# HGRN head: one half chunk of projection taken from behind level 4 and put in front of level 0

## The chip, the cores and the metric

The kernel runs on one core of a Trainium2 chip. The metric is the device time of one execution, in microseconds (us), as the median of several runs. A "head" below is one of the eight HGRN heads, a "half" is half of the matmuls of one chunk of a projection.

## What is computed

The program is one layer of a decoder trunk: RMSNorm, one wide projection of 1024 prompt tokens and 64 sample tokens, dilated attention, HGRN2, causal pooling, gates, and an output projection. The change lies in the HGRN2 part alone. Cut to what matters:

```python
f = lb + (1.0 - lb) * jax.nn.sigmoid(bfg)      # forget gate, 8 heads x 128
logf, kin = jnp.log(f), 1.0 - f
# per head, chunkwise: decay between positions s <= t
decay = exp(cumsum(logf)[t] - cumsum(logf)[s])
att = einsum('btk,btsk,bsk->bts', q, decay, kin)
o = att @ v + (q * exp(A)) @ S                 # S: 128 x 128 state
o_b = rmsnorm(o) * silu(bg)
```

## The kernel before

All tokens lie along the free axis as features x 1088 tokens, in three chunks of 384, 384 and 320 tokens. A projection of one feature block of 128 columns is a *unit*: for each chunk 24 matmuls, since weights and activations are split in a high and a low part (`w_hi` with `x_hi` and `x_lo`, then `w_lo` with `x_hi`). A chunk can be cut in two halves of 12 matmuls; the first half holds the first 12 of them, the second half the other 12, and the third chunk's second half ends the unit.

The weights of a unit are split by GpSimd: a cast into `w_hi` (L206) and a subtraction into `w_lo` (L208), both from SBUF to SBUF, 128x1024 elements. There are two slots, used in turn; GpSimd may split the weights of unit u only when TensorE has finished unit u-2, whose slot they take (the wait on `proj_done` in `split`). So a split starts whenever a unit ends.

A head has four units to project for the *next* head (forget gate, q, v, output gate: `j` = 0 to 3), 24 halves in all, and its own small products: the rows of v transposed (`v_rows`), eight levels of block products (`product(i, n)`, L1341, 34 matmuls of 128x32 in levels 1 to 3 and 32 in levels 4 to 6), the rows of k (`k_rows`), states, outputs, and the transposition back. TensorE runs them in an order written out by hand: `head` places so many halves behind each product. The tuple `counts` says how many: in front of level 0, behind each of the levels 0 to 7, then four numbers for the later places. The queue of every engine is in order.

VectorE serves the levels. Behind the product of level n it runs `update(n)`: it multiplies the decays into `b_block_decay` (L1503), `b_q_decayed` (L1505) and `b_k_decayed` (L1507), and the last of the three releases the product of level n+1. Level 0 has a single multiplication in its place. Then comes `take(n)`, which copies the product out of PSUM (L1486). Between `take(3)` and `update(4)` two more operations stand in VectorE's queue: `b_v_own` (L1527) and `b_q_own` (L1531). All of L1503, L1505, L1507, L1527 and L1531 have both inputs and the output in SBUF; L1486 reads PSUM.

The eight heads are seven turns of a hardware loop and the last head written out by itself, with its own counts.

Of the kernel before, what the change touches and what calls it, by code (L numbers as in the profile page):

```python
# [106 lines left out]
def build(nc, A, OUT):  # L107
    ctx = ExitStack()
    with ctx:
# [1044 lines left out]
        def hgrn_phase(ext, p_gate, p_graw, then):  # L1154
# [10 lines left out]
            with scope:  # L1165
# [71 lines left out]
                with nc.Block() as block:  # L1237
# [86 lines left out]
                    def _(pe):  # L1324
                        def product(i, n):

                            if n == 0:
                                cv.emptied(pe, i * UNITS + 1)
                            pe.wait_ge(level_ready, i * 9 + 1 + n)
                            q = q_new if n == 0 else qp  # L1330
                            for m, (b0, nb, w) in enumerate(level_uses(n)):
                                bank = cv.fill(pe, i * MISC, M[f"p{n}"] + m, w < P or n == LEVELS - 1)
                                for b in range(nb):
                                    t0 = (b0 + b) * P
                                    if n == LEVELS - 1:
                                        mm = pe.matmul(bank[0:HP, b * HP:(b + 1) * HP], kr[:, t0:t0 + HP],
                                                       second(q[:, t0:t0 + P], n), start=True, stop=True)
                                        continue
                                    wq = HP if n == 0 else HP // 2
                                    for r in range(0, w, HP):  # L1340
                                        mm = pe.matmul(bank[r:r + HP, b * wq:(b + 1) * wq], kr[:, t0 + r:t0 + r + HP],  # L1341
                                                       second(q[:, t0 + r:t0 + r + HP], n), start=True, stop=True)
                                mm.then_inc(cv.misc_done, 1)
# [36 lines left out]
                        def outputs(i):  # L1380
                            pe.wait_ge(states_ready, i + 1)
                            for q in range(2):
                                bank = cv.fill(pe, i * MISC, M["o"] + q)
                                for b in range(4):
                                    t = 4 * q + b
                                    mm = pe.matmul(bank[:, b * P:(b + 1) * P], att[:, t, :], vrow[:, t, :],
                                                   start=True, stop=(t == 0))
                                    if t > 0:
                                        mm = pe.matmul(bank[:, b * P:(b + 1) * P], qp[:, t * P:(t + 1) * P],
                                                       state[:, t, :], start=False, stop=True)  # L1390
                                mm.then_inc(cv.misc_done, 1)

                        def back(i):
                            pe.wait_ge(o_ready, i + 1)
                            for q, (b0, nb) in enumerate(spans):
                                bank = cv.fill(pe, i * MISC, M["y"] + q, q == 2)
                                w = P if q < 2 else NS
                                for b in range(nb):
                                    mm = pe.transpose(bank[:, b * P:b * P + w], osb[0:w, b0 + b, :],
                                                      ident[0:w, 0:w])  # L1400
                                mm.then_inc(cv.misc_done, 1)

                        def v_rows(i):
                            cv.emptied(pe, i * UNITS + 2)
                            rows_of(i, v_new, M["v"])

                        def k_rows(i):
                            pe.wait_ge(level_ready, i * 9 + 9)
                            rows_of(i, kr, M["k"])
# [5 lines left out]
                        def head(i, counts):  # L1415

                            halves = [(j, c, half) for j in range(UNITS) for c in range(NCH) for half in range(2)]

                            def meanwhile(n):
                                for j, c, half in halves[:n]:  # L1420
                                    cv.project(pe, i * UNITS + (UNITS + j), j % 2, c, KO, x_hi, x_lo, half=half)
                                del halves[:n]

                            before, levels, own, out, turn, after = counts
                            v_rows(i)
                            meanwhile(before)
                            for n in range(LEVELS):
                                product(i, n)
                                meanwhile(levels[n])
                            k_rows(i)  # L1430
                            meanwhile(own)
                            own_states(i)
                            meanwhile(out)
                            outputs(i)
                            meanwhile(turn)
                            back(i)
                            meanwhile(after)
                            assert not halves

                        with pe.Fori(0, BH - 1) as i:  # L1440
                            head(i, (1, (1, 1, 1, 1, 2, 1, 1, 1), 2, 4, 5, 3))
                        head(BH - 1, (1, (1, 1, 1, 1, 2, 1, 1, 1), 3, 5, 6, 0))
                        for c in range(NCH - 1):
                            cv.project(pe, BH * UNITS + len(POOL_AT), 0, c, KO, x_hi, x_lo)
# [1068 lines left out]
```

## Time and profile before

| | |
|---|---|
| median of 3 runs | 1928.43 us (1927.81 to 1932.0) |
| the profiled execution | 1930.2 us, span 1928.4 us |
| TensorE, matmul records busy | 1886.4 us, 98% of the span |
| VectorE busy | 726.8 us, 38% |
| GpSimd busy | 460.1 us, 24% |
| mean granted TensorE clock | 0.996 |
| the HGRN part | about 715 to 1265 us of the span; one head is 69.2 us |

Idle time is read as follows: a row of a timeline names in brackets how long the engine had stood idle before that group of instructions, and what released it. "issue" means that the profile shows nothing that it waited for. PE is TensorE's matmuls, PEld its weight loads, DVE is VectorE, POOL is GpSimd.

### The profile page before, as it was taken

To read this page: it belongs to the slowest core of one execution; us is meant where nothing else is said; L and a number is where in the kernel's file an instruction comes from. 1 tells how busy PE (TensorE), PEld (TensorE's weight loads), DVE (VectorE), ACT (ScalarE), POOL (GpSimd) and SP (SyncE) were. 2 spreads that over 40 slices of the span, in tenths; PEclk is the share of its full clock that TensorE was granted. 3 is DMA by queue.
4 is the path that set the end of the run, shared out by engine and by line. 5 is a ranking of instruction groups with operands and counts; after the bars stand their busy time and mean duration, and the time that the engine had idled before them with its cause. 6 is when DMAs were issued, how large, how long until landed. Compare 5 with 4: busy or idle time off the path is not lost. (4 is left out here: it accounts for less than half of the span.)

```text
span 1928.4 us, 34551 instructions
## 1 busy us (share of the span) xinstructions
PE 1886.4 (98%) x13648; PEld 1814.0 (94%) x13648; DVE 726.8 (38%) x1271; ACT 355.9 (18%) x876; POOL 460.1 (24%) x266
## 2 busy tenths in 40 slices
PE   7999999999999999999999999999999999999898
PEld 6999998999999999999999999998999999999897
DVE  6223123123222316655755664657200132211523
ACT  5121121122022110111011011122111221111321
POOL 2321222122122121222212222132333333333300
PEclk9999999999999999999999999999999999999999
DMA  5424315322432330221121122123422232212522
GB/s 157 112 68 93 111 53 109 89 74 48 127 92 63 76 94 23 68 67 39 50 67 45 55 66 61 32 79 144 134 68 67 79 103 84 84 56 84 206 89 88
DMA packets 240804, 159.25 MB, mean 83 GB/s; under 512 B 35277, under 2 KB 226125, under 8 KB 240716
## 3 DMA queue, kind: packets, MB, share of 16 engines
q1 hardware_dynamic: 202844, 124.16, 22.7%
q10 hardware_dynamic: 37872, 33.79, 5.3%
q8 instruction: 71, 1.16, 0.3%
q14 instruction: 17, 0.14, 0.0%
HBM read 123.48 MB, written 34.44 MB: 82 GB/s over the span
## 5 line engine op out<-in xcount | busy, mean ns | idle before, releaser
L232 PE MATMUL psum<-x_hi,w_hi 128*128 128x384 f32 (+1 forms) x2496 | 820.8, 334 | 9.6 <-PEq L129 2.8
L232 PE MATMUL psum<-x_lo,w_hi 128*128 128x384 f32 (+1 forms) x2496 | 804.3, 327 | 0.0
L232 PEld LDWEIGHTS psum<-x_hi,w_hi 128*128 128x128 f32 x2496 | 469.9, 188 | 23.5 <-issue 13.8
L232 PEld LDWEIGHTS psum<-x_lo,w_hi 128*128 128x128 f32 x2496 | 470.3, 188 | 0.0
L232 PE MATMUL psum<-x_hi,w_lo 128*128 128x384 f32 (+1 forms) x2496 | 461.3, 326 | 0.0
L206 POOL CAST w_hi<-w_raw 128x1024 fp32r<-128x1024 f32 (+1 forms) x128 | 136.7, 1068 | 1343.7 <-PE psum L232 1063.2
L232 PEld LDWEIGHTS psum<-x_hi,w_lo 128*128 128x128 f32 x2496 | 418.0, 188 | 0.0
L208 POOL TENSOR_TENSOR w_lo<-w_raw,w_hi 128x1024 fp32r<-128x1024 f32 (+1 forms) x128 | 310.4, 2425 | 10.2
L2023 ACT ACTIVATE a_feature<-psum 128x384 f32<-128x384 f32 (+1 forms) x100 | 45.2, 452 | 355.1 <-PE psum L232 355.1
L2135 DVE TENSOR_TENSOR a_prob<-psum,band 128x128 f32<-128x128 f32 (+1 forms) x64 | 21.5, 378 | 204.8 <-PE psum L1829 203.6
L232 PE MATMUL psum<-mb_y_hi,w_hi 128*128 128x384 f32 (+1 forms) x192 | 62.2, 329 | 2.4 <-DVE mb_y_lo L695 2.4
L1341 PEld LDWEIGHTS psum<-b_q_decayed,b_k_decayed 128*64 128x64 f32 x1584 | 51.3, 138 | 12.9 <-issue 8.7
L232 PE MATMUL psum<-mac_y_lo,w_hi 128*128 128x384 f32 (+1 forms) x192 | 62.4, 329 | 0.0
L232 PE MATMUL psum<-mb_y_lo,w_hi 128*128 128x384 f32 (+1 forms) x192 | 62.4, 329 | 0.0
L232 PE MATMUL psum<-mac_y_hi,w_hi 128*128 128x384 f32 (+1 forms) x192 | 62.3, 328 | 0.0
L246 ACT ACTIVATE c_ext<-psum 128x384 f32<-128x384 f32 (+1 forms) x69 | 32.6, 473 | 150.2 <-PE psum L232 146.5
L1486 DVE COPY_PREDICATED b_att<-b_level,psum 64x256 f32<-64x256 int32 (+2 forms) x136 | 58.6, 431 | 2.3
L1341 PE MATMUL psum<-b_q_decayed,b_k_decayed 128*64 128x32 f32 x1584 | 56.6, 224 | 0.7
L1064 DVE TENSOR_TENSOR c_ext<-c_ext,c_gate_raw 128x1088 f32<-128x1088 f32 x7 | 9.9, 1420 | 99.5 <-ACT c_ext L246 99.5
L246 ACT ACTIVATE c_gate<-psum 128x384 f32<-128x384 f32 (+1 forms) x48 | 22.7, 473 | 130.8 <-PE psum L232 95.7
L1064 DVE TENSOR_TENSOR c_ext<-c_ext,c_gate 128x1088 f32<-128x1088 f32 x8 | 11.9, 1493 | 86.5 <-ACT c_ext L246 86.5
L2046 ACT ACTIVATE a_prob<-a_prob,a_stats 128x128 f32<-128x128 f32 (+1 forms) x96 | 41.8, 443 | 0.0
(249 smaller groups left out, 2074.0 us busy)
## 6 DMA issues: line engine op xcount, KB each, us to landing
w_raw<-in_w_in SPq DMA_DIRECT2D x104, 512.0 KB, 3.9
s_cached<-in_cache_kv_w SPq DMA_DIRECT2D x128, 64.0 KB, 2.6
s_cached<-in_cache_kv_w SPq DMA_DIRECT2D x64, 128.0 KB, 2.4
merged_rows<-c_ext ACTq DMA_DIRECT2D x15, 544.0 KB, 3.1
a_feature<-group_weights SPq DMA_DIRECT2D x12, 512.0 KB, 6.2
spare<-branch_outputs SPq DMA_DIRECT2D x10, 544.0 KB, 5.4
branch_outputs<-b_gate ACTq DMA_DIRECT2D x8, 544.0 KB, 3.1
c_ext<-merged_rows SPq DMA_DIRECT2D x8, 544.0 KB, 3.8
```

The source lines that it names most:

```text
L206: pool.tensor_copy(w_hi[:, s, 0:nko, :], w_raw[:, s, 0:nko, :]).then_inc(self.hi_ready, 1)
L208: pool.tensor_tensor(w_lo[:, s, 0:nko, :], w_raw[:, s, 0:nko, :], w_hi[:, s, 0:nko, :].bitcast(F32), ALU.subtract)\
L232: mm = pe.matmul(psum[:, c, 0:n], w[:, s, k, :], x[:, k, t0:t0 + n], start=step is first, stop=step is last)
L246: act.activation(dst[:, t0:t0 + n], psum[:, c, 0:n], func).then_inc(self.bank_free, 1)
L1064: ins = dve.tensor_tensor(pb[p][:, :], pb[p][:, :], gt[p][:, :], ALU.mult)
L1341: mm = pe.matmul(bank[r:r + HP, b * wq:(b + 1) * wq], kr[:, t0 + r:t0 + r + HP], second(q[:, t0 + r:t0 + r + HP], n), start=True, stop=True)
L1486: ins = dve.copy_predicated(dst, msk, src)
L2023: ins = act.activation(by_class(DST[j][:, 0:SEQ], g)[:, :, t0 // STEP[g]:end // STEP[g]], psum[:, c, 0:end - t0].rearrange("p (m r) -> p r ...
L2046: ins = act.activation(prob[:, a:a + w], prob[:, a:a + w], ACT.Exp, bias=st[:, g, c, 0:1], scale=SCALE, accum_out=st[:, g, c, 1:2])
L2135: ins = dve.tensor_tensor(prob[:, a:a + w], ps_, mask, ALU.add)
```

## The change

In the seven looped heads one half is placed in front of level 0 that was placed behind level 4. The number of halves stays 24. The last head keeps its counts.

```diff
                         with pe.Fori(0, BH - 1) as i:
-                            head(i, (1, (1, 1, 1, 1, 2, 1, 1, 1), 2, 4, 5, 3))
+                            head(i, (2, (1, 1, 1, 1, 1, 1, 1, 1), 2, 4, 5, 3))
                         head(BH - 1, (1, (1, 1, 1, 1, 2, 1, 1, 1), 3, 5, 6, 0))
```

The halves themselves keep their order, so those behind levels 0 to 3 are each the next one of the list now. Only TensorE's order changes; the queues of the other four engines hold the same instructions in the same order.

In TensorE's queue, at the front of a head: the rows above the added ones end the first half of the first chunk (unit `j` = 0), L249 and L1329 are the waits of level 0's product.

```order
 L232 MATMUL psum<-x_hi,w_hi 128x384
 L232 MATMUL psum<-x_lo,w_hi 128x384
+L232 MATMUL psum<-x_hi,w_hi 128x384
+L232 MATMUL psum<-x_lo,w_hi 128x384
+L232 MATMUL psum<-x_hi,w_hi 128x384
+L232 MATMUL psum<-x_lo,w_hi 128x384
+L231 REGISTER_ALU
+L232 MATMUL psum<-x_hi,w_lo 128x384 x8
 L249 ISA
 L1329 ISA
```

The second half of the first chunk, 12 matmuls, now runs before level 0's product and not behind it.

In TensorE's queue, between the products of levels 3 and 4: the first L1341 row below is the end of level 3's product, L1329 the beginning of level 4's.

```order
 L1341 MATMUL psum<-b_q_decayed,b_k_decayed 64x32
-L225 REGISTER_ALU
-L232 MATMUL psum<-x_hi,w_hi 128x320
-L232 MATMUL psum<-x_lo,w_hi 128x320
-L232 MATMUL psum<-x_hi,w_hi 128x320
-L232 MATMUL psum<-x_lo,w_hi 128x320
```

```order
+L232 MATMUL psum<-x_hi,w_hi 128x320
+L232 MATMUL psum<-x_lo,w_hi 128x320
+L232 MATMUL psum<-x_hi,w_hi 128x320
+L232 MATMUL psum<-x_lo,w_hi 128x320
+L232 MATMUL psum<-x_hi,w_lo 128x320 x8
 L1329 REGISTER_ALU
```

The first piece begins the rows that leave this place (12 matmuls, the first half of the third chunk), the second is what stands there now: the second half of the third chunk, which ends unit `j` = 0.

In TensorE's queue, behind level 4's product (the L1341 row with 8 matmuls is its end, over the sample tokens); L224 and L225 are the waits of the next unit's first chunk.

```order
 L1341 MATMUL psum<-b_q_decayed,b_k_decayed 64x32 x8
-L232 MATMUL psum<-x_hi,w_hi 128x320
-L232 MATMUL psum<-x_lo,w_hi 128x320
-L232 MATMUL psum<-x_hi,w_hi 128x320
-L232 MATMUL psum<-x_lo,w_hi 128x320
-L232 MATMUL psum<-x_hi,w_lo 128x320 x8
 L224 REGISTER_ALU
 L225 ISA
```

Unit `j` = 0 no longer ends behind level 4's product; the first half of unit `j` = 1 follows that product directly, and it is the only half before level 5's product.

## Rows read from the trace of the kernel before

**Rows 1.** The page, part 1: busy us of each engine, share, instructions

```profile
PE 1886.4 (98%) x13648; PEld 1814.0 (94%) x13648; DVE 726.8 (38%) x1271; ACT 355.9 (18%) x876; POOL 460.1 (24%) x266
```

**Rows 2.** Waits of the weight loads, 700 to 1270 us: total, times, longest

```profile
PEld psum L1341 <- issue: 10.7, 39, 0.4
```

**Rows 3.** Timeline of the weight loads, second head: products of levels 0, 2 to 6

```profile
787.58 1.12 PEld L1341 LDWEIGHTS psum<-b_q_new,b_k_decayed 128*64 128x64 f32 x34 [0.25 <-issue]
...
794.54 1.12 PEld L1341 LDWEIGHTS psum<-b_q_decayed,b_k_decayed 128*64 128x64 f32 x34 [0.28 <-issue]
797.99 1.12 PEld L1341 LDWEIGHTS psum<-b_q_decayed,b_k_decayed 128*64 128x64 f32 x34 [0.25 <-issue]
801.11 1.01 PEld L1341 LDWEIGHTS psum<-b_q_decayed,b_k_decayed 128*64 128x64 f32 x32 [0.19 <-issue]
806.20 1.01 PEld L1341 LDWEIGHTS psum<-b_q_decayed,b_k_decayed 128*64 128x64 f32 x32 [0.25 <-DVE b_att L1486]
809.73 1.02 PEld L1341 LDWEIGHTS psum<-b_q_decayed,b_k_decayed 128*64 128x64 f32 x32 [0.41 <-issue]
```

**Rows 4.** Timeline of PE there: first matmuls of the third chunk's two halves

```profile
799.16 0.42 PE L232 MATMUL psum<-x_hi,w_hi 128*128 128x320 f32 x1
...
802.17 0.41 PE L232 MATMUL psum<-x_hi,w_hi 128*128 128x320 f32 x1
```

**Rows 5.** Timeline of VectorE in the same head, levels 2 to 5

```profile
796.92 0.71 DVE L1507 TENSOR_TENSOR b_k_decayed<-b_k_decayed,b_block_decay 128x544 f32<-128x544 f32 x1
797.56 1.73 DVE L1486 COPY_PREDICATED b_att<-b_level,psum 64x256 f32<-64x256 int32 x3
799.35 0.30 DVE L1503 TENSOR_TENSOR b_block_decay<-b_block_decay 128x136 f32<-128x136 f32 x1
...
800.21 0.72 DVE L1507 TENSOR_TENSOR b_k_decayed<-b_k_decayed,b_block_decay 128x544 f32<-128x544 f32 x1
...
801.85 1.21 DVE L1527 TENSOR_TENSOR b_v_own<-b_v_rows,b_own_row 64x1024 f32<-64x1024 f32 x1
802.98 0.68 DVE L1531 TENSOR_TENSOR b_q_own<-b_q_decayed,b_own_col 128x512 f32<-128x512 f32 x1
...
804.32 0.67 DVE L1507 TENSOR_TENSOR b_k_decayed<-b_k_decayed,b_block_decay 128x512 f32<-128x512 f32 x1
...
807.47 0.94 DVE L1503 TENSOR_TENSOR b_block_decay<-b_block_decay 128x32 f32<-128x32 f32 x1 [1.31 <-PE psum L1341]
...
808.93 0.68 DVE L1507 TENSOR_TENSOR b_k_decayed<-b_k_decayed,b_block_decay 128x512 f32<-128x512 f32 x1
```

**Rows 6.** Timeline of GpSimd in the same head

```profile
804.36 1.54 POOL L206 CAST w_hi<-w_raw 128x1024 fp32r<-128x1024 f32 x1 [16.13 <-PE psum L232]
805.98 2.38 POOL L208 TENSOR_TENSOR w_lo<-w_raw,w_hi 128x1024 fp32r<-128x1024 f32 x1
821.20 1.04 POOL L206 CAST w_hi<-w_raw 128x1024 fp32r<-128x1024 f32 x1 [12.84 <-PE psum L232]
```

**Rows 7.** Timeline of VectorE and of GpSimd in the pooling part, 1297 to 1302 us

```profile
1297.04 1.82 DVE L2424 SCALAR_TENSOR_TENSOR c_pooled<-c_sum,c_ext 128x1024 f32<-128x1024 f32 x1 [0.16 <-DVE c_sum L2418]
1298.78 2.42 DVE L2426 SCALAR_TENSOR_TENSOR c_pooled<-c_sum,c_ext 128x64 f32<-128x64 f32 x1
...
1297.85 3.26 POOL L208 TENSOR_TENSOR w_lo<-w_raw,w_hi 128x1024 fp32r<-128x1024 f32 x1
```

**Rows 8.** Timeline of PE: the two longest gaps behind the first 60 us

```profile
1341.37 0.66 PE L232 MATMUL psum<-x_hi,w_hi 128*128 128x384 f32 x1 [2.77 <-PEq L129]
...
1817.85 0.58 PE L931 MATMUL psum<-w_hi,x_hi 128*128 128x256 f32 x1 [6.57 <-DVE c_ext L1097]
```

**Rows 9.** Stretches behind the first gap: busy times by engine, granted clock, DMA

```profile
1342.00:1344.00 2.00, 2.00 (x8) 2.00 (x7) 1.13 (x1) 2.00 (x3) 0.00 (x0) 0.50 0.71 200
1344.00:1346.00 2.00, 2.00 (x11) 2.00 (x11) 2.00 (x3) 0.83 (x1) 0.29 (x1) 0.82 1.08 397
```

**Rows 10.** One line over all heads: ns min/median/max, first and last start

```profile
L1527 DVE TENSOR_TENSOR b_v_own<-b_v_rows,b_own_row x8: 1207/1209/1210, 732.6 to 1217.0; 64x1024 f32<-64x1024 f32 x8
```

## The prediction

> **What bounds the kernel now.** I read the page's busy times first: TensorE is busy for 98% of the span [rows 1], so whatever doesn't make TensorE wait costs nothing, and whatever makes it wait costs its full length unless a later wait shrinks. Next the waits in the HGRN part. The matmuls have none there, and the weight loads of the levels' products only short ones that nothing releases, 0.4 us the longest [rows 2]. So little can be won there: the reader should see in [rows 3] that each level's product starts with an idle of 0.19 to 0.28 us, which is the ordinary change from one shape to another. One is longer, 0.41 us before level 6: 0.16 us of true waiting. Against that stands what the order protects, and for this I read VectorE's and GpSimd's timelines beside TensorE's.
>
> VectorE is nearly late already. The update of level 2 ends at 796.92 + 0.71 = 797.63 us, that of level 3 at 800.93 [rows 5], and the products of levels 3 and 4, which need them, start at 797.99 and 801.11 [rows 3]: 0.36 and 0.18 us later. The shortest such lag is at level 6, where TensorE does wait: level 5's update ends at 808.93 + 0.68 = 809.61 [rows 5] and the product starts at 809.73, so I take 0.12 us as the cost of the release. From 801.85 to 803.66 VectorE does L1527 and L1531, work that no product waits for, and only then the update of level 4, which ends at 804.32 + 0.67 = 804.99. The product of level 5 starts at 806.20. It's the second half behind level 4 that covers this.
>
> **The change part by part.** No instruction is added or removed, TensorE has the same work, and up to level 5's product the same work stands in front of it in either order. Without waits that product would start at 806.20 as before. All clock times are those of the second head.
>
> *The half in front.* A half of 384 tokens: from level 5's product to level 6's are 3.53 us, less the 0.16 us wait 3.37; the product takes 1.06 of it (801.11 to 802.17, [rows 3, 4]) and the change of shape 0.25, so 2.06 us. Level 0's product, and VectorE's chain behind it, start 2.06 us later. Level 2's update then ends at 797.63 + 2.06 = 799.69, level 3's product starts at 799.81 (its half is one of 320 tokens now, which alone would let it start at 799.72: a wait of 0.1 us).
>
> *Level 4.* VectorE's copies of level 2 ended at 799.29 and end now at 801.35; the update of level 3 takes 1.58 us (799.35 to 800.93, [rows 5]) and ends near 802.88, 1.95 later than before. Level 4's product needs it: 803.00, against 799.81 + 3.12 = 802.93 without the wait. Small.
>
> *Level 5, and the split that moved.* Unit 0 ends before level 4's product now. Its last half starts 1.17 us behind the start of level 3's product (797.99 to 799.16, [rows 3, 4]), so at 800.98; GpSimd started 2.19 us behind the start of that half (802.17 to 804.36, [rows 4, 6]), so now at 803.17. Its cast takes 1.04 us when nothing is in its way [rows 6]: until 804.21. VectorE reaches L1527 at 801.85 + 1.95 = 803.80, while the cast is running.
>
> What happens then? In [rows 5, 6] the 32-column L1503 takes 0.94 us and ends at 808.41, just behind the subtraction's end at 808.36; the cast of 804.36 takes 1.54 us and not 1.04, its last 0.91 us behind the end of L1507 at 804.99. In [rows 7] the subtraction was ready at 1297.85 while L2424 ran until 1298.86, then ran for 2.25 us to 1301.11, and L2426, 64 columns and queued directly behind L2424, ended at 1301.20. So the two engines take turns when VectorE has two SBUF inputs, an instruction at a time, and the one that has waited goes next, also between two back-to-back VectorE instructions.
>
> So: L1527 waits for the cast and ends 1.11 us behind it, at 805.32 (1.21 us less some 0.1 of start-up that the wait hides). The subtraction, ready at 804.29, goes next: 805.32 + 2.25 = 807.57. L1531 waits for it: 0.58 us, 808.15. Level 4's update ends 1.33 us later (803.66 to 804.99, [rows 5]): 809.48. Level 5's product starts at 809.60, not 806.20: 3.40 us late. Less the 0.16 us at level 6, since the subtraction is over by then, 3.24 us in a head. Behind it everything is shifted as a whole, splits too, and TensorE has no other wait that could give it back. All eight heads look alike (L1527 takes 1207 to 1210 ns in each, [rows 10]); seven are changed: 7 x 3.24 = 22.7 us.
>
> The Trainium skill ("SBUF — State Buffer", Who interferes with whom) states that a VectorE instruction with two SBUF inputs and a GpSimd instruction that reads SBUF exclude each other for the whole instruction, and that issue order decides which blocks. The rows above agree (0.94 us where its like take 0.2). No row here shows L1527 itself, on 64 partitions, blocked; by the rule it would be, and the sum would be the 22.7 us; without that it is the first rival's.
>
> *The clock.* The stall leaves the weight loads idle for some 3.5 us in each head. The two longest gaps of the trace, 2.77 and 6.57 us [rows 8], were each followed by the lower level, 1.2 GHz: behind the first it held through 1342 to 1344 us and 0.72 us of the next stretch [rows 9], 3.35 us behind the restart at 1341.37, which costs 1.67 us of work. These are two cases; they don't say how reliably a gap of 3.3 us between full work does it. Bounds: none of seven (0), all seven (11.7 us). I take the middle, 5.8 us, since the new gap is nearer to the shorter of the two.
>
> Sum: 22.7 + 5.8 = 28.5 us. The profiled execution took 1930.2 us around its span of 1928.4; it would take 1958.7. It was 1.8 us above the median of the three runs, which becomes 1956.9.
>
> **Where the costs are nothing.** ScalarE empties the forget gate's chunks earlier; its copies there are hidden by later projections and nothing in the next levels reads them. If that cover were gone, each costs what one copy takes, and TensorE shows no such wait. No transfer is moved in its queue: a load waits for the split two units before, which ends within 1 us of its old time (807.57 against 808.36) and is needed a whole unit later.
>
> **The rivals.**
> 1. *L1527 isn't held up.* The subtraction then starts right behind the cast, 804.29 to 806.68, L1531 ends at 807.26, the update at 808.59, the product starts at 808.71: 2.51 - 0.16 = 2.35 us, 16.5 us in all, with gaps shorter than any that lowered the clock: 1944.9 us. For it: no row shows this form blocked. Against it: it has two SBUF inputs like all that were.
> 2. *No blocking that matters: VectorE keeps its turn through the chain, GpSimd waits.* The update of level 4 ends at 804.99 + 1.95 = 806.94, the product starts at 807.06: 0.86 - 0.16 = 0.70 us, 4.9 us in all: 1933.3; with the cast's 0.4 us 1936. Against it stands L2426 in [rows 7].
> 3. *Every stall lowers the clock.* 22.7 + 11.7 = 34.4 us: 1962.8. For it: both gaps did it. The Trainium skill ("TensorE: Matmul & The Clock Gate", HAM oscillation) tells of a kernel whose recurring waits lowered the clock each time. By that the sum is this one.
> 4. *Not slower.* The backlog behind level 4 isn't there: VectorE starts its chain from a rest before level 0 and gets through L1527, L1531 and the update 0.6 us sooner than shifted rows say, with GpSimd's split falling elsewhere. If level 5's update ends by 806.2, its wait is under the 0.16 us that level 6 gives back: 7 x 0.16 = 1.1 us faster, 1927.3. Against it: VectorE has no idle time between levels 1 and 4 in which it could catch up.
>
> **How the numbers follow.** The exclusive turns with the clock falling in some heads: 0.60, 1956.9, itself between 1951 (no fall) and 1961. Rival 3: 0.20. Rival 1: 0.08. Rival 2: 0.07, of which a third may come out within 0.2% (3.9 us, about what this kernel's measurement can tell from no change), since 4.9 us lies near it. Rival 4: 0.04, within the 0.2% as well. Something else, faster: 0.01. The range runs from 1944, which takes in rival 1, to 1965, which takes in rival 3. Faster 0.01, same 0.06, slower 0.93.
>
> **What the profile will show.** L1341 of level 5 with some 3.5 us of idle before it in seven heads and not in the last; L1531 at more than 2 us and L1527 near 1.5, where they took 0.68 and 1.21; the cast at 1.04 and the subtraction above 3; the 0.41 us before level 6 back at 0.25; stretches at half clock behind the stalls. If L1531 takes 0.68 us, the turn-taking failed and rival 2 holds; if L1527 does not stretch and L1531 does, rival 1. What would make the prediction wrong is mainly the number of falls of the clock, and a split that starts at another time than 803.2.

## The result, and the profile after

The changed kernel takes 1965.9 us (median of 4 runs, 1965.4 to 1966.5) where the kernel before takes 1928.1 us (median of 4): a ratio of 1.0192, interval 1.0174 to 1.0209. It is slower, as forecast, by 37.8 us where 28.5 were forecast, and just above the range that ended at 1965. The profiled execution has a span of 1963.6 us, 35.2 us more than before.

The page of the kernel after, part 1, beside [rows 1]:

```profile
PE 1902.0 (97%) x13648; PEld 1828.2 (93%) x13648; DVE 734.7 (37%) x1271; ACT 356.3 (18%) x876; POOL 473.1 (24%) x266
```

TensorE has the same 13648 matmuls and is busy 15.6 us longer: the same work ran slower somewhere. 15.6 us don't make 35.2; the rest is idle time. The waits of PE over the whole span show it (first the engine that waits and its line, behind the arrow what it waited for, then us in total, times, longest):

```profile
PE psum L1341 <- DVE b_k_decayed L1507: 22.0, 7, 3.1
...
PE psum L232 <- PEq L129: 2.8, 1, 2.8
...
PE psum L232 <- DVE mb_y_lo L695: 0.4, 1, 0.4
```

Seven waits of 3.1 us for L1507, the operation that ends a level's update, one in each of the seven changed heads. The place is level 5's product. The timeline of the weight loads in the second head, which answers to [rows 3], from level 0 to level 6 (with level 1; a row begins with the start and the length of its group):

```profile
794.42 1.12 PEld L1341 LDWEIGHTS psum<-b_q_new,b_k_decayed 128*64 128x64 f32 x34 [0.25 <-issue]
797.90 1.12 PEld L1341 LDWEIGHTS psum<-b_q_decayed,b_k_decayed 128*64 128x64 f32 x34 [0.25 <-DVE b_att L1465]
801.38 1.12 PEld L1341 LDWEIGHTS psum<-b_q_decayed,b_k_decayed 128*64 128x64 f32 x34 [0.28 <-issue]
804.60 1.12 PEld L1341 LDWEIGHTS psum<-b_q_decayed,b_k_decayed 128*64 128x64 f32 x34 [0.29 <-issue]
807.72 1.01 PEld L1341 LDWEIGHTS psum<-b_q_decayed,b_k_decayed 128*64 128x64 f32 x32 [0.19 <-issue]
814.28 0.84 PEld L1341 LDWEIGHTS psum<-b_q_decayed,b_k_decayed 128*64 128x64 f32 x26 [3.45 <-issue]
...
818.87 1.30 PEld L1341 LDWEIGHTS psum<-b_q_decayed,b_k_decayed 128*64 128x64 f32 x32 [0.44 <-issue]
```

Level 5's product starts 6.56 us behind level 4's, where it was 5.09 with one half more between them. The next step, from level 5 to level 6, takes 4.59 us and not 3.37 or 3.53: that is the slower work.

What VectorE and GpSimd did before 814.28 (timelines of the two, beside [rows 5] and [rows 6]):

```profile
806.85 0.71 DVE L1507 TENSOR_TENSOR b_k_decayed<-b_k_decayed,b_block_decay 128x544 f32<-128x544 f32 x1
...
808.50 1.57 DVE L1527 TENSOR_TENSOR b_v_own<-b_v_rows,b_own_row 64x1024 f32<-64x1024 f32 x1
810.00 0.67 DVE L1531 TENSOR_TENSOR b_q_own<-b_q_decayed,b_own_col 128x512 f32<-128x512 f32 x1
810.60 0.21 DVE L1503 TENSOR_TENSOR b_block_decay<-b_block_decay 128x64 f32<-128x64 f32 x1
810.74 0.67 DVE L1505 TENSOR_TENSOR b_q_decayed<-b_q_decayed,b_block_decay 128x512 f32<-128x512 f32 x1
811.34 2.82 DVE L1507 TENSOR_TENSOR b_k_decayed<-b_k_decayed,b_block_decay 128x512 f32<-128x512 f32 x1
...
807.96 1.04 POOL L206 CAST w_hi<-w_raw 128x1024 fp32r<-128x1024 f32 x1 [14.95 <-PE psum L232]
809.08 4.53 POOL L208 TENSOR_TENSOR w_lo<-w_raw,w_hi 128x1024 fp32r<-128x1024 f32 x1
```

L1527 is stretched by the cast (1.57 for 1.21 us). The subtraction was ready at 809.08 and took 4.53 us: VectorE ran through four operations while it waited (L1527, L1531, L1503, L1505), then the subtraction got in, and L1507 took 2.82 us where it had taken 0.67. Its end at 814.16 released the product. The other six changed heads repeat these times to 0.02 us.

The clock behind the stall. The third head's stretches, and the PE rows in them. A row of a stretch has its start and end, its length, the busy times of PE, PEld, DVE, ACT and POOL, then the granted clock (1.00 is 2.4 GHz, 0.50 is 1.2 GHz), the DMA share and GB/s:

```profile
885.00:888.00 3.00, 0.02 (x1) 0.00 (x0) 3.00 (x3) 0.00 (x0) 2.48 (x1) 0.97 0.00 0
888.00:891.00 3.00, 2.85 (x35) 2.79 (x36) 1.90 (x8) 0.00 (x0) 0.00 (x0) 0.50 0.59 175
891.00:894.00 3.00, 3.00 (x11) 2.71 (x9) 1.49 (x3) 0.00 (x0) 0.00 (x0) 0.50 0.00 0
894.00:897.00 3.00, 3.00 (x42) 2.81 (x42) 1.38 (x3) 0.49 (x1) 0.00 (x0) 0.89 0.00 0
```

```profile
888.15 1.92 PE L1341 MATMUL psum<-b_q_decayed,b_k_decayed 128*64 128x32 f32 x32 [3.14 <-DVE b_k_decayed L1507]
...
891.45 2.76 PE L232 MATMUL psum<-x_hi,w_lo 128*128 128x384 f32 x8
```

The granted clock is 0.50, that is 1.2 GHz, for 6.8 us in all (0.18 in the first stretch, 6, 0.66 in the last); the product takes 1.92 us and not 1.13, the eight matmuls 2.76 and not some 1.55. In all seven heads TensorE fell to the lower level at the stall, in the first two for about 3.4 us, in the other five for about 6.8. The first head's stretches, around a product that started at 740.42:

```profile
740.00:742.00 2.00, 1.58 (x33) 1.52 (x34) 1.40 (x6) 0.00 (x0) 0.00 (x0) 0.76 0.32 93
742.00:744.00 2.00, 2.00 (x7) 2.00 (x8) 1.96 (x5) 0.00 (x0) 0.00 (x0) 0.50 0.56 169
744.00:746.00 2.00, 2.00 (x31) 1.74 (x30) 0.32 (x1) 0.49 (x1) 0.00 (x0) 0.89 0.00 0
```

Here the level fell at 741.04, 0.6 us behind the restart, and in the second head 1.8 us behind it. In the five heads with the long spell it fell 0.35 to 0.54 us before the restart, while TensorE still stood idle.

The starts of level 0's product in the second, third and fourth head give the price of a head:

```profile
794.42 1.12 PEld L1341 LDWEIGHTS psum<-b_q_new,b_k_decayed 128*64 128x64 f32 x34 [0.25 <-issue]
868.28 1.12 PEld L1341 LDWEIGHTS psum<-b_q_new,b_k_decayed 128*64 128x64 f32 x34 [0.25 <-issue]
943.48 1.12 PEld L1341 LDWEIGHTS psum<-b_q_new,b_k_decayed 128*64 128x64 f32 x34 [0.25 <-issue]
```

73.86 and 75.20 us, where a head took 69.20. The first two heads cost 4.7 us each and the five others 5.9 to 6.0: 39.0 us for the seven. (The last distance, to the head that wasn't changed, is 2.06 us shorter, a half of 384 tokens; it is counted with that.) The span grew by only 35.2, since the execution profiled before lost nearly 4 us later on that this one didn't: its gap of 2.77 us lowered the clock [rows 8, 9], 1.67 us, and a wait of 2.4 us for L695 followed that is 0.4 us here. After the change a gap of the same kind stands at the same place, and the clock stays up (PE's timeline; the matmul has 0.34 us, at half clock it had 0.52):

```profile
1380.57 0.41 PE L232 MATMUL psum<-x_hi,w_hi 128*128 128x384 f32 x1 [2.78 <-PEq L129]
1380.82 0.34 PE L232 MATMUL psum<-x_lo,w_hi 128*128 128x384 f32 x1
```

This varies from one profiled execution to the next. Over the ten kernels of this document the gap is 2.7 to 2.8 us long every time; the clock fell there in six, and the wait for L695 was 2.4 to 2.5 us in five of these six and 0.4 to 0.5 in the five other executions. Spans can differ by some 4 us for this alone, so the heads are compared by themselves below.

So the question is: is the 3.1 us wait really made by the split together with VectorE's own work, and is everything above it the clock?

### The profile page after: what moved, and what is told of

It is laid out like the page before. It is cut to its first block and busy times, and to the rows that moved or that the text cites. A ratio compares the mean times of both kernels' runs of the same rounds, so it can differ in the third digit from the quotient of the medians.

```text
span 1963.6 us, 34551 instructions
## 1 busy us (share of the span) xinstructions
PE 1902.0 (97%) x13648; PEld 1828.2 (93%) x13648; DVE 734.7 (37%) x1271; ACT 356.3 (18%) x876; POOL 473.1 (24%) x266
## 5 line engine op out<-in xcount | busy, mean ns | idle before, releaser
L232 PE MATMUL psum<-x_hi,w_lo 128*128 128x384 f32 (+1 forms) x2496 | 468.9, 330 | 0.0
L232 PEld LDWEIGHTS psum<-x_hi,w_lo 128*128 128x128 f32 x2496 | 425.3, 191 | 0.0
L208 POOL TENSOR_TENSOR w_lo<-w_raw,w_hi 128x1024 fp32r<-128x1024 f32 (+1 forms) x128 | 326.6, 2551 | 10.3
L1341 PEld LDWEIGHTS psum<-b_q_decayed,b_k_decayed 128*64 128x64 f32 x1584 | 56.5, 149 | 35.7 <-issue 32.9
L1341 PE MATMUL psum<-b_q_decayed,b_k_decayed 128*64 128x32 f32 x1584 | 61.9, 233 | 22.3 <-DVE b_k_decayed L1507 22.0
L1507 DVE TENSOR_TENSOR b_k_decayed<-b_k_decayed,b_block_decay 128x512 f32<-128x512 f32 (+1 forms) x48 | 48.2, 1004 | 0.0
L246 ACT ACTIVATE c_gate<-psum 128x384 f32<-128x384 f32 (+1 forms) x48 | 22.7, 473 | 130.8 <-PE psum L232 95.7
```

What stands on the lines that cost most here:

```text
L208: pool.tensor_tensor(w_lo[:, s, 0:nko, :], w_raw[:, s, 0:nko, :], w_hi[:, s, 0:nko, :].bitcast(F32), ALU.subtract)\
L232: mm = pe.matmul(psum[:, c, 0:n], w[:, s, k, :], x[:, k, t0:t0 + n], start=step is first, stop=step is last)
L246: act.activation(dst[:, t0:t0 + n], psum[:, c, 0:n], func).then_inc(self.bank_free, 1)
L1507: dve.tensor_tensor(kv[:, :, 0, :], kv[:, :, 0, :], fv[:, :, 1:2].broadcast_to([P, nb, half_]), ALU.mult)\
```

## The experiments

Eight kernels. "Per head" is the distance from one head's level 0 to the next one's in the profiled execution, less the 69.20 us of the kernel before (where the last head is the unchanged one, 2.06 us are added for its shorter front). The four from late_split to level4_to_own ran with one set of runs of the kernel before (median 1929.95 us), the four below them with another (1929.72 us).

| kernel | median us | ratio (interval) | per head, us |
|---|---|---|---|
| the change | 1965.92 | 1.0192 (1.0174 to 1.0209) | 4.7 twice, 5.9 to 6.0 five times |
| late_split | 1931.13 | 1.0015 (1.0001 to 1.0028) | 0.64 |
| filler | 1951.70 | 1.0111 (1.0092 to 1.0131) | 3.13 |
| front_from_own | 1938.45 | 1.0047 (1.0033 to 1.0061) | 1.58 |
| level4_to_own | 1943.41 | 1.0073 (1.0052 to 1.0095) | 2.11 |
| own_later | 1949.72 | 1.0099 (1.0080 to 1.0118) | 1.6 twice, 3.1 five times |
| filler4 | 1960.12 | 1.0155 (1.0129 to 1.0181) | 3.1 five times, 4.6 twice |
| own_later_late_split | 1935.66 | 1.0026 (1.0014 to 1.0038) | 0.47 |
| before_late_split | 1929.24 | 0.9995 (0.9984 to 1.0005) | -0.15 |

**late_split: the split out of the way.**

```diff
                             for j in range(UNITS):
                                 cv.split(pool, i * UNITS + (SLOTS + j), j % 2, i * (UNITS // 2) + (1 + j // 2), KO)
+                            pool.wait_ge(level_ready, i * 9 + 9)
```

> The changed kernel, with one wait more in GpSimd's queue: at the end of each turn it waits for the update of level 7 before it begins the split that unit 0's end used to release. Theory (the split gets between VectorE's operations in front of level 5's product): without it only VectorE's own backlog is left, level 5's product waits 0.6 to 0.9 us in a head, L1507 takes 0.68 us again, the clock stays up: 1933 us, within 2. Rival (VectorE's backlog alone makes the 3.1 us wait and the split is a bystander): 1966 us as the changed kernel, with the 3.1 us wait in place.

Measured: 1931.1 us, 0.15% above the kernel before, as expected. Of the 3.1 us wait 0.63 are left, and no head lost its clock. Its lines are numbered one higher. VectorE's and PE's timelines:

```profile
803.63 1.21 DVE L1528 TENSOR_TENSOR b_v_own<-b_v_rows,b_own_row 64x1024 f32<-64x1024 f32 x1
...
806.10 0.68 DVE L1508 TENSOR_TENSOR b_k_decayed<-b_k_decayed,b_block_decay 128x512 f32<-128x512 f32 x1
...
806.91 1.12 PE L1342 MATMUL psum<-b_q_decayed,b_k_decayed 128*64 128x32 f32 x32 [0.63 <-DVE b_k_decayed L1508]
```

VectorE's own work, which the rival held for the cause, makes only this 0.63 us. The order of TensorE is that of the changed kernel to the instruction, so the order by itself costs these 0.6 us in a head, and the rest of the 5.6 us that a head lost on average comes with the moved split. In sum 0.64 us are 4.5 us for seven heads, while the medians differ by 1.2; the ten runs spread from 1929.6 to 1938.0 us, and the profiled one was among the fastest and didn't have the later loss of 4 us.

**filler: the stall kept, the clock held up.**

```diff
                                 product(i, n)
                                 meanwhile(levels[n])
+                                if n == 4 and before == 2:
+                                    bank = cv.fill(pe, i * MISC, M["p5"])
+                                    for k in range(16):
+                                        pe.matmul(bank[:, 0:384], w_hi[:, 1, k % KO, :], x_hi[:, k % KO, 0:384],
+                                                  start=True, stop=True)
```

> The changed kernel with 16 matmuls of 384 columns more behind the half that follows level 4, in seven heads; their result is overwritten by level 5's product and read by nothing. They take 2.8 us of the 3.1 us in which TensorE waited. Theory (35 us are 22 us of waiting and 13 us of half clock behind it): the clock stays at 2.4 GHz through the heads and the time is 1928 + 22 = 1950 us, within 2. Rival (the slow stretch behind the stall is not from the clock's fall on idle time, or the fillers delay the product as much as they save): 1964 to 1968 us.

Measured: 1951.7 us, within the expected 1950 by 2. PE's timeline in the second head (lines behind the new loop are numbered five higher), and the stretch behind the first head's stall:

```profile
808.36 2.94 PE L1433 MATMUL psum<-x_hi,w_hi 128*128 128x384 f32 x16
811.64 1.12 PE L1341 MATMUL psum<-b_q_decayed,b_k_decayed 128*64 128x32 f32 x32 [0.34 <-DVE b_k_decayed L1512]
```

```profile
740.00:746.00 6.00, 6.00 (x72) 5.44 (x68) 4.68 (x12) 0.49 (x1) 0.00 (x0) 1.00 0.31 91
```

The product starts as late as before: 6.55 us behind level 4's. But the clock stays at 1.00, here and in every other head, and a head costs 3.13 us, every one of them. Useless matmuls made the changed kernel 14 us faster. With this the parts of the change are measured apart: 7 x 3.13 = 21.9 us of stall, and above that 2 x 1.55 and 5 x 2.8, 17.1 us, for the clock.

**front_from_own: the same collision, one half more to cover it.**

```diff
-                            head(i, (2, (1, 1, 1, 1, 1, 1, 1, 1), 2, 4, 5, 3))
+                            head(i, (2, (1, 1, 1, 1, 2, 1, 1, 1), 1, 4, 5, 3))
```

> The half in front of level 0 is taken from behind the rows of k and not from behind level 4: two halves in front, two behind level 4, one fewer behind the rows of k. Unit 0 ends before level 4's product as in the changed kernel, so the split meets VectorE's chain at the same place, but level 5's product is due one half (2.06 us) later. Theory: the wait there is 3.1 - 2.06, about 1.1 us, the clock stays up, less the 0.16 us at level 6: 1935 us, within 2.5. Rival (what costs is only that one half is missing behind level 4): no wait, 1928. Rival (the half in front itself costs): the 3.1 us stay, 1950 or more.

Measured: 1938.5 us, 8.5 more than before and 1 us above what was expected. The weight loads of levels 5 and of the states:

```profile
811.45 1.02 PEld L1341 LDWEIGHTS psum<-b_q_decayed,b_k_decayed 128*64 128x64 f32 x32 [1.42 <-issue]
...
824.24 1.86 PEld L1359 LDWEIGHTS psum<-b_v_rows,b_k_rows 128*128 128x128 f32 x16 [0.49 <-DVE b_k_rows L1515]
```

The wait at level 5 is the 1.1 us of the expectation; L1507 was stretched to 2.86 us as in the changed kernel. The half missing behind the rows of k opened a wait at L1359, 0.49 us of idle before the weight loads, that I had not seen coming, and that is why a head costs 1.58 and not 1.1 us. The two waits leave nothing for a cost of the half in front of level 0 by itself.

**level4_to_own: the front as before, one half less behind level 4.**

```diff
-                            head(i, (2, (1, 1, 1, 1, 1, 1, 1, 1), 2, 4, 5, 3))
+                            head(i, (1, (1, 1, 1, 1, 1, 1, 1, 1), 3, 4, 5, 3))
```

> The second half behind level 4 is moved back, behind the rows of k, and the front of the head keeps one half. Unit 0 ends behind level 4's product as before the change. Theory: level 5's product waits 0.9 us for VectorE, then the subtraction of the split (805.98 to 808.36 in the second head of the kernel before) stands in front of level 5's update, so that level 6's product can start no sooner than before, 809.7, with one half less done: 2.06 us in a head, 14.4 us, 1942.5 us, within 3, no fall of the clock. Rival (any kernel with one half behind level 4 behaves like the changed one): 1962 to 1968 us.

Measured: 1943.4 us, 2.11 us in a head (2.06 were expected). The weight loads of levels 5 and 6 and level 5's update:

```profile
807.22 1.02 PEld L1341 LDWEIGHTS psum<-b_q_decayed,b_k_decayed 128*64 128x64 f32 x32 [1.20 <-issue]
811.83 1.02 PEld L1341 LDWEIGHTS psum<-b_q_decayed,b_k_decayed 128*64 128x64 f32 x32 [1.52 <-issue]
```

```profile
808.48 2.02 DVE L1503 TENSOR_TENSOR b_block_decay<-b_block_decay 128x32 f32<-128x32 f32 x1 [0.22 <-PE psum L1341]
```

The split (its subtraction ran from 808.07 to 810.45) meets level 5's update, as in the kernel before, but a half's time earlier in TensorE's order. There are two waits, of 1.2 and 1.5 us before the weight loads (0.94 and 1.20 us before the matmuls), neither followed by the lower clock.

**own_later: VectorE's other work taken out of the chain.** L1527 and L1531 move behind the copies of the rows of k.

```diff
-                            ch.step(dve.tensor_tensor(vown[:, :, :], ...))
-                            dve.wait_ge(level_ready, i * 9 + 5)
-                            dve.tensor_tensor(qown[:, :, :], ...).then_inc(own_ready, 1)
                             for n in range(4, LEVELS):
                                 update(n)
                                 take(n)
...
                             rows_to(krow, M["k"])
+                            ch.step(dve.tensor_tensor(vown[:, :, :], ...))
+                            dve.wait_ge(level_ready, i * 9 + 5)
+                            dve.tensor_tensor(qown[:, :, :], ...).then_inc(own_ready, 1)
```

> The changed kernel with b_v_own (L1527) and b_q_own (L1531) taken out of VectorE's queue between take(3) and update(4) and put behind the copies of the rows of k. Theory (1.8 us of VectorE's own work and 2.2 us of the split stand in front of level 5's product): only one of the two is left. If the split's subtraction, ready 1.1 us after the cast starts, goes in ahead of part of update(4), level 5's product waits up to 2 us: 1928 to 1942 us; if VectorE runs through its chain first, as it did through four operations in the changed kernel, update(4) ends before the product is due and the wait is gone: 1927 to 1929 us. Rival (the split alone makes the wait, whatever VectorE has to do): 3.1 us remain, 1960 us or more.

Measured: 1949.7 us, above the 1942 that was the upper end. VectorE, GpSimd and PE in the second head, and the stretches behind its restart:

```profile
809.09 0.23 DVE L1503 TENSOR_TENSOR b_block_decay<-b_block_decay 128x64 f32<-128x64 f32 x1 [0.40 <-PE psum L1341]
809.23 2.89 DVE L1505 TENSOR_TENSOR b_q_decayed<-b_q_decayed,b_block_decay 128x512 f32<-128x512 f32 x1
...
809.19 2.38 POOL L208 TENSOR_TENSOR w_lo<-w_raw,w_hi 128x1024 fp32r<-128x1024 f32 x1
...
812.85 1.13 PE L1341 MATMUL psum<-b_q_decayed,b_k_decayed 128*64 128x32 f32 x32 [1.59 <-DVE b_k_decayed L1507]
```

```profile
812.00:816.00 4.00, 3.15 (x39) 3.11 (x40) 3.65 (x11) 0.00 (x0) 0.00 (x0) 0.77 0.46 131
816.00:820.00 4.00, 4.00 (x46) 3.64 (x45) 1.41 (x4) 0.49 (x1) 0.00 (x0) 0.81 0.00 0
```

The subtraction went in directly behind L1503, and the wait was 1.59 us with the split alone, where it was 0.63 with VectorE's own work alone (late_split) and 3.14 with both. The two alone make 2.2: the missing 0.9 us is the cover that TensorE has at this place, which each of them can use by itself, but both together only once (an estimate, as if the two delays simply add). What I missed is the clock: although the gap is only 1.6 us, it fell in five heads of seven, each time 1.2 to 1.9 us behind the restart, and cost 1.5 us each time. 7 x 1.6 + 5 x 1.5 = 18.7 us in the heads, where the medians differ by 20.0.

**filler4: four fillers for sixteen.** The loop `for k in range(16)` becomes `range(4)`.

> The kernel with fillers, but with 4 matmuls of 384 columns in place of 16: 0.7 us of the 3.1 us gap is filled and 2.4 us stay idle, 22 us of delay in all as in both neighbours. Theory: the time lies between 1950 (the clock stays up in all heads) and 1966 (it falls in all), and the part above 1950 is half of the TensorE work done at half clock; a gap of 2.4 us seldom lowers it: 1953 us. Rival (the fillers gained by something other than the clock, in proportion to their number): 1962 us with no spell at half clock.

Measured: 1960.1 us, between the neighbours, from four runs that lie far apart: 1952.7 and 1957.6 us with a mean granted clock of 0.994, 1962.6 and 1962.9 us with 0.986 and 0.987. The waits of PE in the profiled execution (the one of 1957.6):

```profile
PE psum L1341 <- DVE b_k_decayed L1512: 16.7, 7, 2.4
```

This gap lowered the clock in two heads, which took 73.8 us, while the five others, with the same four fillers, took 72.3, as with sixteen. A head's time goes with the clock and not with the number of fillers: the rival, which had no spell at half clock, is out. My 1953 was too low a guess of how often it falls. In the two slowest runs, which were not profiled, the mean clock says that it fell more often.

**own_later_late_split: both causes removed.** The edits of own_later and of late_split together.

> Both: the two operations behind the rows of k, and GpSimd's split held until the update of level 7. Theory: nothing stands in front of level 5's product, and level 6's 0.16 us is gone: 1927 us, within 1.5 of the kernel before. Rival (the single half behind level 4, or the half in front, has a cost of its own): 1932 or more.

Measured: 1935.7 us, 0.26% above the kernel before. There is no wait left at the levels, but a new one at L1366, for the moved operation (lines one higher; VectorE, GpSimd, the waits of PE):

```profile
821.32 1.21 DVE L1536 TENSOR_TENSOR b_v_own<-b_v_rows,b_own_row 64x1024 f32<-64x1024 f32 x1
822.45 2.85 DVE L1540 TENSOR_TENSOR b_q_own<-b_q_decayed,b_own_col 128x512 f32<-128x512 f32 x1
...
820.98 3.78 POOL L208 TENSOR_TENSOR w_lo<-w_raw,w_hi 128x1024 fp32r<-128x1024 f32 x1
...
PE psum L1366 <- DVE b_q_own L1540: 3.4, 7, 0.5
```

The moved split found the moved operation: L1540 took 2.85 us for 0.68. Half a microsecond in a head, 3.3 us in all, and this wait is all that the heads lose, so the rival (a cost of the order by itself) finds nothing there. The rest up to the measured 5.9 isn't explained by this profile: it is of the second fastest of the twelve runs, which spread from 1931.1 to 1939.0 us and may or may not have had the later loss of some 4 us. So the expectation failed, by the same mechanism at another place.

**before_late_split: the kernel before with the split held back.** The edit of late_split alone.

> The kernel before with GpSimd's split held until the update of level 7, and nothing else. Theory: L1503 of level 5's update takes 0.2 us and not 0.94, the 0.16 us wait in front of level 6's product goes, eight times: 1.3 us faster, 1927 us, which the measurement may not tell from nothing. Rival (the later split makes the weights or VectorE's L1539 late): slower by 2 us or more.

Measured: 0.9995, interval 0.9984 to 1.0005. A head is 0.15 us shorter, which is the 0.16 us wait before level 6; the measurement can't tell it from no change. No kernel here beats the one before clearly.

## Why the prediction failed by its size

**Right: where and why TensorE stalls.** The step from level 0 to level 5 was forecast as 19.96 us and came out as 19.86; the split was forecast to start 13.53 us behind level 0 and started 13.54 behind it. The stall's price was forecast as 3.24 us in a head and filler measured 3.13. late_split shows that the split is necessary for it, own_later that VectorE's own work is the other cause. Rival 2 (no blocking) forecast 0.70 us in a head for what late_split then was: 0.64.

**Wrong in detail: who goes next.** The step "the one that has waited goes next" failed. L1531 was not held up at all (0.67 us); VectorE kept its turn for four operations in a row while the subtraction waited 2.3 us, and L1507 was the one that lost. It made no difference for the end, since all of it lies in front of L1507's end in any order: that the stall came out right in spite of the wrong turn is luck of this place. The prediction's own sign was set wrongly by it: "If L1531 takes 0.68 us, the turn-taking failed and rival 2 holds". L1531 took 0.67 us, and rival 2, with its 0.70 us in a head, didn't hold. L1527 was held by the cast, so rival 1 is out. One small sum doesn't close: 801.35 + 1.58 us is 802.93 and not 802.88, which moves nothing.

**Wrong: the clock.** This is the step that failed. The term was 5.8 us, the middle between no fall and seven falls of 1.67 us. Measured are seven falls and 17.1 us. Both halves of the estimate were too low. How often: I chose the middle, where the two longest gaps known had both lowered the clock; it fell seven times of seven. The rows of before couldn't show how it falls with another length or at another place: the gap before the merging part lowered the clock in six profiled executions of ten. How much: I took the price of one fall from [rows 9], 3.35 us at half clock, as an upper bound. Five of the seven lasted about 6.8 us and cost 2.8 us each. The gap of 6.57 us in [rows 8] has such a longer spell behind it, also of 6.8 us, of which 4.7 us lie behind the restart; I hadn't read its stretches. Rival 3, all seven falling, was nearest with 1962.8 us, and too low for the second reason alone.

The Trainium skill ("TensorE: Matmul & The Clock Gate", HAM oscillation) tells of a kernel whose wait in every tile cost the clock each time. The changed kernel's trace agrees, with seven of seven; own_later (five of seven) and filler4 (two of seven) have a wait that recurs just so and don't lose the clock each time.

The sum now: 21.9 us of stall and 17.1 us of clock are 39.0 us in the heads, less about 4 us that the profiled execution of before lost elsewhere, against 35.2 us in the spans. The medians differ by 37.8 us. The prediction had 22.7 and 5.8.

## What to carry to other kernels

In an order written out by hand, look at what an engine's progress releases on the others. Here the costly instruction was on neither TensorE's nor VectorE's list of changes: GpSimd's weight split starts when a projection unit ends, and a half moved ahead of level 4 put that end in front of the tightest chain. Price a stall of TensorE of more than a microsecond with the clock, from every spell of half clock that the trace shows and not from one; here the clock cost nearly as much again as the stall. A kernel with fillers in the gap measures the two apart.

## What the runs showed of the hardware

The length of the idle gap alone doesn't say whether the clock falls. Gaps of 3.1 us lowered it in seven heads of seven (the changed kernel) and gaps of 1.6 us in five of seven (own_later), but gaps of 2.4 us only in two of seven (filler4), two gaps of 0.9 and 1.2 us in each head never (level4_to_own), and the gap of some 2.8 us ahead of the merging part did it in six profiled executions of ten. One fall cost between 1.5 and 2.8 us in the same program. The dear ones in the changed kernel are those that fell before TensorE restarted (0.35 to 0.54 us before, spells of 6.8 us); all that fell behind the restart, here, in own_later and in filler4, lasted 3.4 us. A fall before the restart isn't enough for a long spell, though: behind gaps of 2.4 to 2.8 us in the merging part some came 0.05 to 0.5 us before it (the kernel before, front_from_own, filler, filler4) and lasted 3.4 us. What decides it stays open.

In these traces GpSimd's subtraction and VectorE's instructions with two SBUF inputs take turns, but not in the order in which they ask. The subtraction got in behind one operation of VectorE when it had waited 0.1 us (own_later) and when it had waited 1.0 us [rows 7], and only behind four when it had waited 2.3 us (the changed kernel, front_from_own). In own_later_late_split it is recorded from 820.98 and took 3.78 and not 2.38 us, yet L1536, which began at 821.32, ran at full speed. The Trainium skill ("SBUF — State Buffer", Who interferes with whom) says that who issues first gets the pair of ports that the two engines share, for the whole instruction; where L1505 (own_later), L1507 and L1540 were held up, the trace agrees; where L1531, L1503 and L1505 passed a waiting subtraction in the changed kernel, it doesn't. What decides it stays open.
